# Shift products of the opening turned round: the condition's column stationary, the modulation's blocks moving

## The reference, cut to what matters

```
c_act = silu(c)                                   # c: 1 x 1024
mod = c_act @ ada_w[0] + ada_b[0]                 # 1 x 6144
sh1, sc1, g1, sh2, sc2, g2 = split(mod, 6)        # 1024 each
hn = rms_norm(h, norm1_g[0]) * (1 + sc1) + sh1    # 512 x 1024
z = hn @ lru_w_in[0]                              # first big product
```

## Time and profile before

| | us |
|---|---|
| median of 3 runs | 2520.79 (2518.05 to 2523.57) |
| the profiled execution | 2517.27 |
| its span in the profile | 2515.5 |
| PE busy | 2491.1 (99%) |
| DVE busy | 1433.2 (57%) |
| ACT busy | 1130.0 (45%) |

### The profile page before, as it was taken

One profiled execution on the slowest core, in us unless ns is written; L12 is line 12 of the kernel. 1 busy time (PEld: TensorE's weight loads), 2 busy tenths in 40 slices (PEclk: granted clock), 3 DMA queues, 4 the chain that ended last, 5 costly groups with the idle time before them and its releaser, 6 DMA issues.

```text
span 2515.5 us, 32916 instructions
## 1 busy us (share of the span) xinstructions
PE 2491.1 (99%) x12330; PEld 1985.5 (79%) x12330; DVE 1433.2 (57%) x2227; ACT 1130.0 (45%) x2015; POOL 25.9 (1%) x18
## 2 busy tenths in 40 slices
PE   9999999999999999999999999999999999999999
PEld 7887888888777788888877777778877777777887
DVE  7987656567667653433456644554475664455435
ACT  6675523433546442443445544442354554444234
POOL 0000000000000000000000000000020000000002
PEclk9999999999999999999999999999999999999999
DMA  7633456665221123222221211222322121122233
GB/s 300 216 109 134 168 203 207 205 206 191 84 92 62 57 84 107 95 101 92 96 106 68 76 59 64 84 72 92 106 87 101 68 76 64 62 80 74 91 109 109
DMA packets 77903, 280.38 MB, mean 111 GB/s; under 512 B 8640, under 2 KB 8896, under 8 KB 77504
## 3 DMA queue, kind: packets, MB, share of 16 engines
q1 hardware_dynamic: 61056, 219.60, 24.8%
q10 hardware_dynamic: 16704, 58.79, 6.8%
HBM read 276.26 MB, written 2.10 MB: 111 GB/s over the span
## 4 chain that ended last, share of the span: by engine, by line
PE 93%; DVE 4%; ACT 2%; DMA 1%; issue 1%; ACTq 0%; SPq 0%; DVEq 0%
PE ps L222 26%; PE ps L224 25%; PE ps L223 25%; PE ps L1832 2%; PE ps L1919 2%; PE ps L1892 1%; PE ps L1735 1%; DVE wl L217 1%; PE ps L1836 1%; PE ps L1226 1%; PE ps L1792 1%; PE ps L1153 1%; PE ps L1206 1%; PE ps L2016 1%; ACT wh L214 1%; PE ps L1181 1%
## 5 line engine op out<-in xcount | busy, mean ns | idle before, releaser
L217 DVE TENSOR_TENSOR wl<-raw,wh 128x1024 fp32r<-128x1024 f32 x372 | 456.9, 1228 | 621.5 <-ACT wh L214 621.5
L222 PE MATMUL ps<-xh,wl 128*128 128x512 f32 x1744 | 696.5, 399 | 8.1 <-DVE wl L217 3.9
L224 PE MATMUL ps<-xh,wh 128*128 128x512 f32 x1744 | 680.8, 390 | 0.0
L223 PE MATMUL ps<-xl,wh 128*128 128x512 f32 x1744 | 680.3, 390 | 0.0
L214 ACT ACTIVATE wh<-raw 128x1024 fp32r<-128x1024 f32 x372 | 392.8, 1056 | 624.7 <-PE ps L224 613.9
L222 PE MATMUL ps<-bh,wl 128*128 128x512 f32 x1174 | 463.6, 395 | 3.6 <-DVE bl L1388 1.9
L224 PE MATMUL ps<-bh,wh 128*128 128x512 f32 x1174 | 457.3, 390 | 0.0
L223 PE MATMUL ps<-bl,wh 128*128 128x512 f32 x1174 | 457.1, 389 | 0.0
L222 PEld LDWEIGHTS ps<-xh,wl 128*128 128x128 f32 x1744 | 327.3, 188 | 127.7 <-issue 44.6
L224 PEld LDWEIGHTS ps<-xh,wh 128*128 128x128 f32 x1744 | 327.7, 188 | 70.4
L223 PEld LDWEIGHTS ps<-xl,wh 128*128 128x128 f32 x1744 | 327.8, 188 | 65.2 <-issue 1.2
(11 more groups left out here) (327 smaller groups left out, 2535.7 us busy)
## 6 DMA issues: line engine op xcount, KB each, us to landing
raw<-in_w SPq DMA_DIRECT2D x388, 512.0 KB, 3.2
bA<-in_ada ACTq DMA_DIRECT2D x74, 512.0 KB, 4.5
bC<-in_ada SPq DMA_DIRECT2D x9, 512.0 KB, 12.6
bD<-in_ada ACTq DMA_DIRECT2D x8, 512.0 KB, 4.9
bS<-in_attn_bias ACTq DMA_DIRECT2D x8, 512.0 KB, 3.2
bD<-in_ada SPq DMA_DIRECT2D x7, 512.0 KB, 14.9
bC<-in_ada ACTq DMA_DIRECT2D x6, 512.0 KB, 4.2
h<-in_x SPq DMA_DIRECT2D x4, 512.0 KB, 7.4
```

The costliest lines, as they stand in the source:

```text
L217: e.tensor_tensor(wl[p][:], raw[p][:], wh[p][:].bitcast(F32), ALU.subtract)\
L222: e.matmul(out, wl[p][:, blk, 0:M], xhi, start=start, stop=False)
L223: e.matmul(out, wh[p][:, blk, 0:M], xlo, start=False, stop=False)
L224: return e.matmul(out, wh[p][:, blk, 0:M], xhi, start=False, stop=stop)
```

## The change

The turned product has the condition's column as the stationary operand (128 x 1) and the block of 128 x 128 as the moving one (128 columns), so it yields a row of 128 shifts on one partition. ACT copies the row to the part of bC or bD that is free, PE turns it into a column with a matmul of one row by a one, and ACT reads that column as before. All eight shifts are done so; DOT_TILES is empty. On ACT the copy of row k + 1 stands ahead of the instructions of tile k; on PE `behind(kt)` puts the column of tile kt + 2 behind the third passes of tile kt. Two more idle passes stand ahead of column 1.

```
--- before.py
+++ after.py
@@ -62,7 +62,7 @@
 ADA_FIRST = 16
 ADA_SLOTS = 14
 ADA_MLP = 18
-DOT_TILES = (3, 6)
+DOT_TILES = ()
 
 
 VEC = {}
@@ -492,7 +492,7 @@
                         put_lo(s, k - 1, y, shift, hi, lo)
                 put_lo(s, n - 1, y, shift, hi, lo)
 
-            def first_pair(u0, used, s, hi, lo, tiles=range(KD), between=lambda kt: None):
+            def first_pair(u0, used, s, hi, lo, tiles=range(KD), between=lambda kt: None, behind=lambda kt: None):
 
                 if pe:
                     for q in range(2) if tiles[0] == 0 else ():
@@ -514,6 +514,7 @@
                                 done(mm, f"{s}half{q}")
                             if kt == KD - 1:
                                 mm.then_inc(s_unit, 1)
+                        behind(kt)
 
             def split_first(u, s, q):
 
@@ -671,19 +672,35 @@
                 if pe and m < KD and m not in DOT_TILES:
                     if m == 0:
                         need("i_cc")
-                    if m >= 4 and m - 4 not in DOT_TILES:
+                    if m >= 4:
                         need(f"n0sh{m - 4}")
                     e.wait_ge(s_a0[2 * m], 16)
                     for kt in range(KD):
-                        mm = e.matmul(ps[2 + m % 4][:, 0:1], early_slots[2 * m % ADA_SLOTS][:, P * kt:P * kt + P], c_col[:, kt:kt + 1],
+                        mm = e.matmul(ps[2 + m % 4][0:1, 0:P], c_col[:, kt:kt + 1], early_slots[2 * m % ADA_SLOTS][:, P * kt:P * kt + P],
                                       start=kt == 0, stop=kt == KD - 1)
                     done(mm, f"i_ada{2 * m}")
+                if act:
+                    need(f"i_ada{2 * m}")
+                    done(e.activation(shift_row(m), ps[2 + m % 4][0:1, 0:P], ACT.Copy), f"n0row{m}")
+
+            def shift_row(m):
+
+                return (bC, bD)[m // 4][0:1, 10, P * (m % 4):P * (m % 4) + P]
+
+            def shift_column(m):
+
+                if pe and m < KD:
+                    need(f"n0row{m}")
+                    done(e.matmul(ps[2 + m % 4][:, 0:1], shift_row(m), ones[0:1, 0:1], start=True, stop=True), f"n0col{m}")
 
             if pe:
                 idle_passes(2, 6)()
                 shift_product(0)
                 idle_passes(4, 6)()
+                shift_column(0)
                 shift_product(1)
+                idle_passes(2, 6)()
+                shift_column(1)
             if act:
                 for q in range(2):
                     e.wait_ge(s_raw[q], 16)
@@ -697,21 +714,20 @@
                     e.tensor_tensor(wl[q][:], raw[q][:], wh[q][:].bitcast(F32), ALU.subtract).then_inc(s_lo, 1)
             nsp2 = acc
 
+            if act:
+                shift_product(0)
             for k in range(KD):
-                if dve:
-                    shift_product(k)
+                if act and k + 1 < KD:
+                    shift_product(k + 1)
+                if dve:
                     if k:
                         e.wait_ge(s_a0[2 * k + 1], 16)
                         done(ada_dot(early_slots[(2 * k + 1) % ADA_SLOTS], sm[:, SNM + k:SNM + k + 1]), f"i_ada{2 * k + 1}")
                     if 0 < k < KD - 1:
                         done(e.tensor_tensor(bT[:, k + 1, :], h[:, k + 1, :], ps[7][:], ALU.mult), f"n0r{k + 1}")
                 if act:
-                    need(f"i_ada{2 * k}")
-                    if k in DOT_TILES:
-                        i = e.activation(mod[:, k:k + 1], sm[:, SNM + KD + k:SNM + KD + k + 1], ACT.Identity, bias=v("ada_b", k))
-                    else:
-                        i = e.activation(mod[:, k:k + 1], ps[2 + k % 4][:, 0:1], ACT.Identity, scale=0.5, bias=v("ada_b", k))
-                    done(i, f"n0sh{k}")
+                    need(f"n0col{k}")
+                    done(e.activation(mod[:, k:k + 1], ps[2 + k % 4][:, 0:1], ACT.Identity, scale=0.5, bias=v("ada_b", k)), f"n0sh{k}")
                     need(f"i_ada{2 * k + 1}")
                     done(e.activation(gs[:, 0, k:k + 1], sm[:, SNM + k:SNM + k + 1], ACT.Identity,
                                       scale=v("norm1_g", k), bias=mod[:, KD + k:KD + k + 1]), f"n0gs{k}")
@@ -748,7 +764,8 @@
                         e.dma_start(raw[p][:], io["w"][2 * i + (2 + p)]).then_inc(s_raw[p], 16)
 
 
-            first_pair(0, BK, "n0", xh, xl, between=lambda kt: shift_product(kt + 2))
+            first_pair(0, BK, "n0", xh, xl, between=lambda kt: shift_product(kt + 2),
+                       behind=lambda kt: shift_column(kt + 2))
             for q in range(2):
                 split_first(2 + q, "n0", q)
```

## The result

The changed kernel takes 2540.06 us in the median of four runs (2537.99 to 2543.74), the kernel before 2522.11 beside it: ratio 1.0082, 95% interval 1.0067 to 1.0096, so 18 us slower. In a second series it was 2544.36 against 2519.40, ratio 1.0097 (1.0067 to 1.0128). The forecast was 2539.

A forecast was written before the change was run, and what follows sets the result against it. PE is busy for 99% of the span, but the opening, up to DVE's convolution, sets the program's end. Later high part 7 less what returns gives +16.1, clock +2: 2520.8 + 18.1 = 2539 us, range 2532 to 2553.

The forecast's parts named there:

- The serial cycle: Opening, PE and ACT: product, row copy and tile run one behind another, 5.39 us a tile for tiles 1 to 6.
- High part to row copy: From ACT's high part through PE's passes and next product until ACT copies the row: 2.92 us plus 0.04 for the signal.
- shift to high part: ACT's own work on one tile, from the shift's start to the high part's end: 2.18 us, unchanged.
- The product's price: Turned product on PE costs the same as the old one, bounds -0.3 to +0.3 us a product.
- Case 4: Rival, chance 0.04: not slower; one-column stationary operand halves a record, PE takes 2.6 us a tile; 2520.8 us.
- case 3: Rival, chance 0.05: the row copy isn't in the tile's way, PE bounds at 3.4 us a tile; +5 us, 2526.
- The row copy: New copy on ACT from PSUM: 0.27 us by the nearest row, 0.29 with signal, bounds 0.2 to 0.6.
- The two dots: Taking two dots (2.3 us) from DVE is worth nothing: 2.35 us of work a tile in a 5.4 us period.
- What comes back: Behind high part 7, units 2 and 3 have landed, so DVE's convolution starts after 2.75 instead of 3.9 us: gain 1.15.
- The signs that I had named for the convolution: Trace signs: DVE's convolution first at 62 to 65 us instead of 46.6, PE's later wait at about 88 to 90.
- The clock: PE's clock in the opening falls to about half at times: +2 us taken, bounds 0 and 16.5.
- The rule on the clock: Skill page: the gate follows how busy the array has been; read strictly, pauses put the opening at half clock.

The follow-up runs named there:

- the second trace: The changed kernel run again with no edit, to get a second profile; median 2544.36 us, ratio 1.0097 to the kernel before.
- the run with the row behind: Changed kernel with ACT's copy of row k + 1 moved behind tile k, all instructions kept; 2530.71 us, ratio 1.0036 to the kernel before.
- Filling the pauses: Changed kernel with six idle passes of 512 columns on PE behind each column from tile 2 on; 2538.21 us, ratio 1.0064 to the kernel before.
- the kernel before without dots: Kernel before with all eight shifts as old products (DOT_TILES empty), nothing else changed; 2528.01 us, ratio 1.0029 to the kernel before.
- the dots back and 22 passes: Changed kernel with row copy behind tile k, shifts 3 and 6 as DVE dots, 22 idle passes at the start; 2521.21 us, ratio 0.9999.
- the run with the wait: Kernel before with all eight shifts as old products, and ACT waiting for product k + 1 ahead of tile k; 2554.02 us, ratio 1.0132.

## Why the prediction was right

**The serial cycle** was right and is shown: moving one line gives back 13.7 us with the load unchanged, and the wait without any turned product costs about 26 us by the ratios (1.0132, against 1.0029 for the two dots as products alone). Predicted 5.39 us a tile at full clock, measured 5.45 to 5.52. High part to row copy is 3.12 us (38.23 to 41.35 in the second trace) where I had 2.92 and 0.04 for the signal: the product takes 0.07 more and starts 0.10 later behind the passes. The row copy holds ACT for 0.17 us where I had 0.25, and shift to high part is 2.16 (2.18).

**The product's price**: 1.91 us against 1.84, within the bounds of 0.3. A weight load of one column (84 ns against 192) spares nothing: the product's records follow each other at the pace of their moving columns, as in the earlier trace rows. Case 4 falls with that row. Once PE is the bound, though, a tile costs more than the 3.4 us of case 3: 3.93 in the run with the row behind, 0.31 of it the column.

**The row copy**: 0.27 us for 1 x 128, as the nearest row gave.

**The two dots** were costed rightly as worth nothing for DVE. That they came to stand in the serial chain on PE is 6.9 of the loss; it was in my sum as two of the six periods, but not named.

**What comes back** behind high part 7: 1.15 us predicted; 0.99 in the first trace (73.47 - 70.54 = 2.93 against 3.92), 0.1 in the second, where the clock was low for the last tile. The signs that I had named for the convolution (62 to 65 us) and for PE's wait behind it were missed for that and for the slow tiles: it starts at 73.5 and 70.7.

**The clock** is the term that was mis-sized. I took +2 us near the low end of 0 to 16.5. In the second trace, which has no slow start, high part 7 ends at 66.9 against 59.9 forecast. Of these 7.0 us, 0.6 are the start, 0.4 the slightly longer period, and 6 the four slow tiles; with the last tile and the first pair the clock cost 7. Filling the pauses gave 6 back. In the first trace the start took 5 us more on top. That the first series still met the forecast, with +18.0 against +18.1, is partly luck: the second gave +25.0, and the medians of before moved too, 2522.11 in one and 2519.40 in the other. The mechanism was right and the clock's term too small by some 5 us.

**The rule on the clock** that I had weighed is that the gate follows how busy the array has been (the Trainium skill, "TensorE: Matmul & The Clock Gate", Part 1). The profile's busy time alone doesn't give it here. Both rows are from 22.5 to 30 us, with PE busy for 7.50 of 7.50 us, first the kernel before without dots, with old products (one moving column), then the one with the row behind, with turned ones (128):

```profile
22.50:30.00 7.50, 7.50 (x28) 6.82 (x29) 5.38 (x9) 3.33 (x7) 0.00 (x0) 0.50 1.03 411
22.50:30.00 7.50, 7.50 (x47) 4.79 (x45) 4.98 (x10) 5.01 (x11) 0.00 (x0) 1.00 1.03 410
```

It is tempting to say that the turned product holds the clock better. In the traces with the same serial order the clock is indeed 0.82 against 0.50, and the medians are 9.7 us apart (2544.36 and 2554.02), but the intervals of their ratios overlap (1.0067 to 1.0128, 1.0104 to 1.0161), and from 34 to 44 us the kernel without dots ran its old products at 1.00. So this isn't shown. What is shown is that it brought no gain: the kernel with the row behind, at 1.00 from 30 us on in both traces, is slower than the kernel before (1.0036), and with the dots back and 22 passes level with it (0.9999).

## What to carry to other kernels

Before adding a step to an engine that works in order, ask what the new instruction waits for and what already stands behind it: a copy of 0.27 us put ahead of a tile cost more than 10 us, because it waited for work that this same tile's predecessor releases. A lookahead lives in the order of two engines, and one early read on one of them ends it. And when a chain of waits names a transfer, ask what else ends at the same time before moving the transfer.

## What the runs showed of the hardware that was not expected

- PE can be busy without a pause and yet at half clock: 7.50 of 7.50 us at 0.50, in a stretch with products of one moving column. In the run with the wait the clock was 0.50 over 45 us; with 128 moving columns and the same order 0.82, and 1.00 with the pauses filled. It isn't a rule of the one column: the same products ran at 1.00 from 34 to 44 us in the kernel without dots.
- The same program has executions in which PE falls to half clock at 12 to 14 us and stays there to about 24. It was seen in four of the twelve traces and costs 5 us and more (high part 0 at 31.0 against 26.0; the convolution at 57.9 against 52.4). The untraced runs point the same way: the granted clock on record for a whole run of the kernel before is 0.996 to 0.997 at 2517 to 2519 us and 0.991 to 0.993 above 2527, though none of those slower runs was traced. What starts it stays open.
- A matmul of one row by one element takes 0.38 us in two records, and an ACT copy of 1 x 128 from PSUM as long (0.27 us) as one of 128 x 128.
